# Making the operand parts of the memory attention's output product inside the attention's last rounds

## The reference, cut to what matters

```
o = einsum('bhsm,bmhd->bshd', softmax(q @ k^T / 16), v).reshape(b, s, 1024)
x = x + o @ w_xo
h = rmsnorm(x, norm_ffn_w);  x = x + square(relu(h @ w_ff1)) @ w_ff2
```

## Time and profile before

| what | value |
|---|---|
| median of 3 runs | 4275.41 us (4272.5 to 4280.73) |
| the profiled execution's own time | 4270.85 us |
| its span, first to last instruction | 4269.5 us |
| mean granted TensorE clock | 0.941 |
| PE busy | 3925.1 us, 92% of the span, 33542 matmuls |
| DVE, ACT, POOL busy | 2143.8, 1157.7 and 330.9 us |
| HBM read and written | 215.54 MB and 58.43 MB |

### The profile page before, as it was taken

One profiled execution on the slowest core, in us unless ns is written; L12 is line 12 of the kernel. 1 busy time (PEld: TensorE's weight loads), 2 busy tenths in 40 slices (PEclk: granted clock), 3 DMA queues, 4 the chain that ended last, 5 costly groups with the idle time before them and its releaser, 6 DMA issues. The chain is left out here.

```text
span 4269.5 us, 75519 instructions
## 1 busy us (share of the span) xinstructions
PE 3925.1 (92%) x33542; PEld 3213.0 (75%) x33542; DVE 2143.8 (50%) x3526; ACT 1157.7 (27%) x1598; POOL 330.9 (8%) x362
## 2 busy tenths in 40 slices
PE   6999959988989999999999899777887999999999
PEld 5788837777867888888798677566666788888877
DVE  4633345555434444454624332555554476666773
ACT  4221234433313221212400322343323321111132
POOL 0001102231000000000000000232311000000000
PEclk8999969998999999999999899888788999999999
DMA  5212120113112111111232312311004211111111
GB/s 180 88 52 70 50 84 6 32 32 132 40 59 89 50 41 49 49 50 50 68 118 97 125 60 84 86 35 45 22 10 163 96 50 40 60 40 50 50 45 64
DMA packets 212888, 278.83 MB, mean 65 GB/s; under 512 B 15548, under 2 KB 170940, under 8 KB 212436
## 3 DMA queue, kind: packets, MB, share of 16 engines
q1 hardware_dynamic: 181040, 201.84, 14.8%
q10 hardware_dynamic: 31524, 72.16, 4.5%
HBM read 215.54 MB, written 58.43 MB: 64 GB/s over the span
## 5 line engine op out<-in xcount | busy, mean ns | idle before, releaser
L436 PE MATMUL ps<-sb_a_h,sb_whi 128*128 128x512 f32 x2784 | 1107.3, 398 | 2.9 <-DVE sb_wlo L397 2.4
L438 PE MATMUL ps<-sb_a_h,sb_whi 128*128 128x512 f32 x2784 | 1090.7, 392 | 0.0
L437 PE MATMUL ps<-sb_a_h,sb_wlo 128*128 128x512 f32 x2784 | 1090.4, 392 | 0.0
L436 PEld LDWEIGHTS ps<-sb_a_h,sb_whi 128*128 128x128 f32 x2784 | 526.1, 189 | 130.8 <-issue 16.1
L437 PEld LDWEIGHTS ps<-sb_a_h,sb_wlo 128*128 128x128 f32 x2784 | 526.6, 189 | 112.7 <-issue 4.6
L438 PEld LDWEIGHTS ps<-sb_a_h,sb_whi 128*128 128x128 f32 x2784 | 525.8, 189 | 112.7
L389 ACT ACTIVATE sb_whi<-sb_wraw 128x2048 fp32r<-128x2048 f32 (+3 forms) x146 | 260.4, 1783 | 826.0 <-PE ps L438 500.6
L397 DVE TENSOR_TENSOR sb_wlo<-sb_wraw,sb_whi 128x2048 fp32r<-128x2048 f32 (+3 forms) x146 | 315.1, 2158 | 237.0 <-ACT sb_whi L389 216.4
L548 DVE TENSOR_TENSOR sb_x<-sb_x,ps 128x512 f32<-128x512 f32 x480 | 313.8, 685 | 216.1 <-PE ps L438 207.4
L436 PE MATMUL ps<-sb_a_g,sb_whi 128*128 128x512 f32 x896 | 349.7, 390 | 10.5 <-DVE sb_x L548 10.5
L437 PE MATMUL ps<-sb_a_g,sb_wlo 128*128 128x512 f32 x896 | 348.7, 389 | 0.0
(11 more groups left out here) (525 smaller groups left out, 5806.1 us busy)
## 6 DMA issues: line engine op xcount, KB each, us to landing
sb_wraw<-w_in SPq DMA_DIRECT2D x33, 1024.0 KB, 5.3
sb_wraw<-w_ff SPq DMA_DIRECT2D x32, 1024.0 KB, 5.3
sb_wraw<-w_up SPq DMA_DIRECT2D x22, 1024.0 KB, 5.1
sb_wraw<-w_down SPq DMA_DIRECT2D x11, 1024.0 KB, 4.9
sb_wraw<-w_xkv SPq DMA_DIRECT2D x8, 1024.0 KB, 5.6
sb_wraw<-w_out SPq DMA_DIRECT2D x8, 1024.0 KB, 5.5
gates<-sb_a_f ACTq DMA_DIRECT2D x32, 256.0 KB, 2.0
sb_a_f<-gates SPq DMA_DIRECT2D x32, 256.0 KB, 4.8
```

The lines of the kernel that those rows point to most:

```text
L436: e.matmul(o, wh[:, k, c], xh[:, sl], start=(k == 0), stop=False)
L437: e.matmul(o, wl[:, k, c], xh[:, sl], start=False, stop=False)
L438: m = e.matmul(o, wh[:, k, c], xl[:, sl], start=False, stop=(k == t.nk - 1))
```

## The change

The round trip through HBM and the meeting of the engines between attention and output product are taken apart. For heads 0 to 2 (feature blocks 0 to 5) the outputs still go to `xo`, but SP now reads them back (`sp_xo`), as soon as the last queries are made: each block lands in the place of its own low part (`raw(k)`). In rounds 8, 9 and 10 ACT makes two high parts each, and DVE two low parts in place. For head 3 (blocks 6 and 7) ACT and DVE make the parts straight from PSUM, in halves of 512 tokens, and nothing is written to HBM. `pe_first` becomes a generator: PE runs 24 of its 96 matmuls at the end of round 9, 24 at the end of round 10, and the rest after it. `next_phase()` is gone, and the first four tiles take banks 0, 2, 3 and 4, after which `RING` goes on from bank 5.

```diff
-        def pe_first(e, tiles, x, ready, feats=None, side=None, at=None):
+        def pe_first_steps(e, tiles, x, ready, feats=None, side=None, at=None, ring=None):
...
-            ps = [bk.take(t.key, RING) for t in tiles]
+            ps = [bk.take(t.key, ring or RING) for t in tiles]
...
+                yield
             wend[j] = bk.filled(tiles[-1].key)
...
+            xos = abreast_last(fm("xo", "w_xo", 0, 1024))
+            first_steps = []
+            def raw(k):
+                return R(H0 + (8 + k) * T, T)
+            def xo_ready(k):
+                return llo.at(8 + k) if k < 6 else bk.emptied(("xa_o", 7, k - 6))
+            HIGHS = [0, 1, (6, 0), (6, 1), 2, 3, (7, 0), (7, 1), 4, 5]
+            def xo_high(what):
+                return lhi.at(8 + HIGHS.index(what))
...
+                if r == 9:
+                    first_steps.append(pe_first_steps(e, xos[:4], hp, xo_ready, None, None, None, (0, 2, 3, 4)))
+                    bk.spot[RING] = 5
+                if r >= 9:
+                    for _ in range(2):
+                        next(first_steps[0])
...
+                    else:
+                        for dv in range(2):
+                            hi, lo = (x[:, span(u % 2)] for x in hp(6 + dv))
+                            e.wait_ge(*xo_high((u, dv)))
+                            e.tensor_tensor(lo, bk["xa_o", u, dv], hi.bitcast(F32), ALU.subtract).then_inc(*bk.empty(("xa_o", u, dv)))
...
+                if r >= 8:
+                    for k in (2 * r - 16, 2 * r - 15):
+                        e.wait_ge(*xo_high(k))
+                        e.tensor_tensor(hp(k)[1], raw(k), hp(k)[0].bitcast(F32), ALU.subtract).then_inc(*llo.up())
...
+                        if u >= 6:
+                            e.wait_ge(*bk.filled(("xa_o", u, dv)))
+                            e.activation(hp(6 + dv)[0][:, span(hf)], bk["xa_o", u, dv], ACT.Copy).then_inc(*lhi.up())
+                            continue
...
+                if r >= 8:
+                    e.wait_ge(*lp[r - 8].at(2))
+                    for k in (2 * r - 16, 2 * r - 15):
+                        e.activation(hp(k)[0], raw(k), ACT.Copy).then_inc(*lhi.up())
+            def sp_xo(e):
+                e.wait_ge(*bk.filled(asks[7][-1].key))
+                for k in range(6):
+                    for x in xo_out:
+                        e.wait_ge(*x.at(k // 2 * 2 + 1))
+                    e.dma_start(raw(k), S["xo"][k * 128:(k + 1) * 128, :]).then_inc(*lp[k // 2].up())
...
             sp_load(sp, asks[-1][0].j + 3)
-            next_phase()
+            sp_xo(sp)
...
-                pe_first(e, xos[:4], hp, llo.at)
+                for _ in first_steps[0]:
+                    pass
...
-                ve_parts(e, 8, hp, bufs)
...
-                ac_parts(e, S["xo"], 8, hp, bufs)
```

More of the change, by code:

```diff
@@ L596, in pe_first @@
                         m.then_inc(*bk.fill(t.key))
+                yield
             wend[j] = bk.filled(tiles[-1].key)
+        def pe_first(e, *args):
+            for _ in pe_first_steps(e, *args):
+                pass
         def ac_high_piece(e, q, n, seg, gain):
@@ L2198, in ve_xa @@
                 if 0 <= u < UNITS:
-                    e.wait_ge(*bk.filled(("xa_o", u, 0)))
-                    e.wait_ge(*xo_out[0].at(u - 1))
-                    e.tensor_copy(xob[0], bk["xa_o", u, 0]).then_inc(*bk.empty(("xa_o", u, 0)))
+                    if u < 6:
+                        e.wait_ge(*bk.filled(("xa_o", u, 0)))
+                        e.wait_ge(*xo_out[0].at(u - 1))
+                        e.tensor_copy(xob[0], bk["xa_o", u, 0]).then_inc(*bk.empty(("xa_o", u, 0)))
+                    else:
[3 more added lines that the diff above has]
+                            e.tensor_tensor(lo, bk["xa_o", u, dv], hi.bitcast(F32), ALU.subtract).then_inc(*bk.empty(("xa_o", u, dv)))
                 u = r - 1
@@ L2233, in ac_xa @@
                     h, hf = divmod(u, 2)
-                    e.wait_ge(*bk.filled(("xa_o", u, 1)))
-                    e.wait_ge(*xo_out[1].at(u - 1))
-                    e.activation(xob[1], bk["xa_o", u, 1], ACT.Copy).then_inc(*bk.empty(("xa_o", u, 1)))
+                    if u < 6:
+                        e.wait_ge(*bk.filled(("xa_o", u, 1)))
+                        e.wait_ge(*xo_out[1].at(u - 1))
+                        e.activation(xob[1], bk["xa_o", u, 1], ACT.Copy).then_inc(*bk.empty(("xa_o", u, 1)))
                     for dv in range(2):
+                        if u >= 6:
+                            e.wait_ge(*bk.filled(("xa_o", u, dv)))
+                            e.activation(hp(6 + dv)[0][:, span(hf)], bk["xa_o", u, dv], ACT.Copy).then_inc(*lhi.up())
+                            continue
                         row = (2 * h + dv) * 128
@@ L2245, in a2 @@
             sp_load(sp, asks[-1][0].j + 3)
-            next_phase()
-            xos = abreast_last(fm("xo", "w_xo", 0, 1024))
+            sp_xo(sp)
             def ffn_gain(k):
```

## The result

The changed kernel took 4258.93 us in the median (12 runs, 4252.62 to 4272.19) against 4273.65 us for the kernel before (12 runs, 4264.11 to 4285.9), a ratio of 0.9968 with a 95% interval of 0.9956 to 0.998. The forecast was 4267.0 us within 4262 to 4273. The median of the first measurement lies 3.1 us under that range, that of the second inside it.

A forecast was written before the change was run, and what follows sets the result against it. The prediction took PE's 10.31 us idle on write, meet, read, high, low, plus a slow-clock stretch, as the bound; 10.4 us gained less 2.0 for the clock gave 8.4 off 4275.4, so 4267.0 us, range 4262 to 4273.

The forecast's parts named there:

- What bounds the kernel: Between attention and output product: PE idles 10.31 us on write, meet, read, high, low; then 2.4 us lost at low clock.
- a gain comes through: Behind the first four product tiles PE runs from 1308.3 to 2085 us without a wait, so nothing swallows an earlier end.
- Step 1: Read-backs of blocks 0 to 3, issued before 1250 us, have over 13 us until 1263.9 and cost nothing.
- Steps 2 and 3: Rounds 8 and 9: parts queued first empty bank 7 late; unit 6's second output tile starts 2.6 us later, gap about 3.4.
- Steps 4 to 6: Bursts of 24, 24 and the rest, with a 1.5 us gap in round 10; at full clock the tiles end 10.4 us earlier.
- Step 7: The 3.4 us PE gap halves the granted clock for one slow stretch, costing 2.0 us, between bounds of 1.5 and 2.4.
- How the numbers follow: Split of the chances: faster 44, same 50, slower 6; 0.2% (8.6 us) taken as about what a measurement can tell from no change.
- The clock did not hold: Rival: the granted clock stays 1.00 through PE's gap; gain 10.4 us, 4265.0 us; chance 15%.
- nor did the low clock last: Rival: the clock stays low over all 96 matmuls of the first four tiles; 8.8 us slower, 4284.2 us; chance 3%.
- The operand was not late: Rival: SP's six read-backs miss their time and PE waits at a burst; 4272 to 4278 us; chance 3%.
- The bank rotation gave nothing back: Rival: RING's new position makes later stages' tiles wait, bounded by 4 us either way, mostly a loss; 4270.5 us; chance 14%.

The follow-up runs named there:

- e8: The changed kernel with the last head also sent through HBM (units 6 and 7 written, blocks 6 and 7 read back); ratio 0.9976 to the kernel before.
- e5: The changed kernel with the halves of unit 6's block 6 made ahead of the parts of blocks 0 and 1; ratio 0.9958 to the kernel before.
- e1: The kernel before with only the bank rotation RING moved on by four places behind the output product; 4278.86 us, ratio 1.0009 to the kernel before.
- e7: The changed kernel with all 96 matmuls behind the attention and the meeting of all engines put back before them; ratio 0.9993 to the kernel before.
- e2: The changed kernel measured again, nothing altered; 4266.44 us against 4274.57 for the kernel before, ratio 0.9976.
- e3: The changed kernel without its two early bursts, all 96 matmuls behind the attention's last output tile; ratio 0.9974 to the kernel before.
- e4: The changed kernel with block 6's halves of unit 6 made first and bank 1 for units 6 and 7's second output tiles; ratio 0.995 to the kernel before.
- e6: The changed kernel with block 6's halves first, output tiles alternating banks 7 and 3 and queries on two banks in all rounds; ratio 0.9956 to before.

## Why the prediction was right or wrong

**What bounds the kernel, and that a gain comes through** were right. The gap of 10.31 us is gone, no wait stands between the seam and the next stage, and the 720.0 us of work behind it are as long as before.

**Step 1, the read-backs** was right: ACT never waits for a DMA there, and e8 shows that even the last head's would have been in time.

**Steps 2 and 3, the late bank 7** were right in mechanism (e5), 0.35 us too large: output tile (6,1) starts 5.9 us after the transposes, forecast 6.3. The forecast held ACT's first high part until 1263.92, 1.53 us behind the transposes, where the copy L2230 stood; it starts at 1.20. The queue alone would have let both go at 1.16, where ACT has issued its two writes, so the copy must have waited for the transposes as well. PE's gap was 3.01 us for 3.4.

**Steps 4 to 6** were right within 0.5 us together, and the gap of 1.41 us stood where 1.5 had been forecast; forecast and measured agree on 18.2 to 18.4 us from (7,1) to the end.

**Step 7, the clock** fell as forecast, once, and came back. It cost 1.6 us (e5) where 2.0 were taken: the lower bound had been nearer. The reason given, a gap of 3.43 us that halved the clock and one of 2.25 that did not, was too thin: the trace of the kernel before also has 0.50 behind gaps of 2.30 us (at 496.66) and 2.26 us (at 2453.43). That the clock fell and came back once was therefore right with some luck.

The three errors point the same way and add up: 0.35, 0.5 and 0.4 us are the 1.2 us between the 8.4 forecast for the seam and the 9.6 measured.

**The step that failed is "How the numbers follow".** The mechanism and the seam were right; the term that was mis-sized is the scatter. The range gave the runs' own scatter 2 to 3 us and took the median of three runs of before for its level. The 12 runs of before spread over 21.8 us and those of the change over 19.6, and two medians of the changed kernel lie 7.5 us apart, 4258.93 outside the range and 4266.44 inside it, 0.6 us from the forecast. Of the 8.1 us between forecast and first median the seam explains 1.2 and the level of before 1.8 (4273.65 for 4275.41); the rest is scatter. By these numbers the range should have reached some 5 us further to both sides, which is an estimate. The argument that 0.2% cannot be told from no change was wrong too: both intervals leave out 1, with gains of 0.32% and 0.24%.

**The rivals.** The clock did not hold, nor did the low clock last. The operand was not late. The bank rotation gave nothing back and brought nothing that e1 could show; its interval spans 11.5 us, so an effect of 2 or 3 us in the later stages would not show in the total.

## What to carry to other kernels

Before a round trip through HBM is taken away, ask what makes it visible. Here the same trip cost nothing once it was started early and nobody met behind it (e8), and a meeting put back cost 7.8 us with no transfer to wait for (e7). Work that is moved into an earlier round is paid by whoever stands behind it in the queue: put what empties the next PSUM bank first and the parts of the later product second, since the gap of 3.01 us in front of PE was paid twice here, once idle and once at half clock (e5). Where a kernel's total scatters by 20 us, read a change of 10 us in its own stretch of the trace.

## What the runs showed of the hardware

- Behind a PE gap of 3.01 us the granted clock was halved in all five traces that have it here (changed, e2, e3, e7, e8), behind gaps of 1.41 and 1.27 us in none of e4, e5 and e6. The low stretch cost 1.6 us in the changed kernel. In e7 it lasted over output tile (7,0) too, which took 3.75 us for 1.95 in e3.
- One and the same gap of 2.26 us was followed by 0.50 in the kernel before and by 1.00 in the changed one, worth 2.6 us.
- At a granted clock of 1.00 the same work took 720.0 us in eleven of twelve traces; where the clock changed, the same 6246 matmuls took 385.2 to 397.6 us. Up to the same matmul at 1260 to 1271 us executions differ by 10.8 us.
- Transfers beside it did not slow ACT's making of a pair of high parts: 2.00 us at 1268.20, where the DMA share was 0.53, and 2.00 us at 1277.02, where it was 0.11.
